# Ten landing slots, later accumulating transfers and a re-ordered DMA queue in the output product of a feed-forward block

## What is computed

```python
def conv_ffn(x, g_norm, w_in, conv_w, conv_b, w_out):
    h = rms_norm(x, g_norm)
    hu = causal_depthwise_conv(h @ w_in, conv_w, conv_b)
    gate, up = jnp.split(hu, 2, axis=-1)
    return (jax.nn.silu(gate) * up) @ w_out
...
        x = x + conv_ffn(x, f_norm[layer], f_w_in[layer], f_conv_w[layer], f_conv_b[layer],
                         f_w_out[layer])
```

## Time and profile before

| what | value |
|---|---|
| median of 3 runs | 2029.73 us (2027.12 to 2032.08) |
| the profiled execution, its own time | 2034.66 us |
| its span | 2032.9 us |
| mean granted TensorE clock | 0.98 |
| TensorE matmuls, share of the span | 96% |
| VectorE / ScalarE / GpSimd | 74% / 46% / 22% |
| output product of layer 0 (first to last matmul start) | 752.74 to 978.61 us |
| output product of layer 1 | 1804.32 to 2029.35 us |

### The profile page before, as it was taken

The page is one execution under the profiler, slowest core; times in us unless marked ns, Lnnn a source line. Parts: engine busy times, 40 slices in busy tenths (PEclk is TensorE's granted clock), DMA queues, the critical chain, the costliest instruction groups (busy, mean ns, idle before and its releaser), DMA issues.

```text
span 2032.9 us, 27966 instructions
## 1 busy us (share of the span) xinstructions
PE 1947.5 (96%) x9704; PEld 1649.4 (81%) x9704; DVE 1503.0 (74%) x2202; ACT 933.9 (46%) x1620; POOL 445.5 (22%) x321
## 2 busy tenths in 40 slices
PE   7999899999999998999999799989999999989999
PEld 7988778788888886888999688867788888867887
DVE  5356658888888875786844688889887887866875
ACT  5233434544444443444412788756444444433443
POOL 0000001333333220020110445532333333310100
PEclk9999999999999998999999799999999999999999
DMA  4111142122222259680112000011222222289761
GB/s 170 43 42 42 52 155 104 62 83 83 83 82 83 83 174 311 192 207 1 42 42 69 15 11 12 22 78 68 84 83 83 83 83 83 83 240 339 142 143 63
DMA packets 62820, 198.99 MB, mean 98 GB/s; under 512 B 5008, under 2 KB 5136, under 8 KB 55568
## 3 DMA queue, kind: packets, MB, share of 16 engines
q1 hardware_dynamic: 48080, 163.29, 22.6%
q0 software_dynamic: 14656, 34.61, 7.9%
HBM read 162.22 MB, written 35.65 MB: 97 GB/s over the span
## 4 chain that ended last, share of the span: by engine, by line
PE 80%; DVE 10%; DMA 4%; ACT 3%; issue 1%; SPq 0%; POOL 0%; DVEq 0%; ACTq 0%
PE banks L2082 26%; PE banks L2084 26%; PE banks L2083 26%; DMA raw<-in_w_f_out 1%; DMA b<-c_scratch 1%; DVE t_lo L1600 1%; DMA c_scratch<-xT 1%; ACT lg L1302 1%; PE banks L2418 1%; DVE t_sum L1840 1%; DVE t_sum L1590 1%; DVE lg L1982 1%; DVE small L1989 1%; DVE fw_lo L1756 1%; DVE xT L1682 1%
## 5 line engine op out<-in xcount | busy, mean ns | idle before, releaser
L2082 PE MATMUL banks<-t_hi,fw_hi 128*128 128x512 f32 x1248 | 488.8, 392 | 11.0 <-issue 11.0
L2084 PE MATMUL banks<-t_hi,fw_lo 128*128 128x512 f32 x1248 | 486.9, 390 | 0.0
L2083 PE MATMUL banks<-t_lo,fw_hi 128*128 128x512 f32 x1216 | 474.6, 390 | 0.0
L2082 PEld LDWEIGHTS banks<-t_hi,fw_hi 128*128 128x128 f32 x1248 | 235.5, 189 | 61.3 <-issue 12.6
L2084 PEld LDWEIGHTS banks<-t_hi,fw_lo 128*128 128x128 f32 x1248 | 235.2, 188 | 49.3
L2083 PEld LDWEIGHTS banks<-t_lo,fw_hi 128*128 128x128 f32 x1216 | 229.4, 189 | 48.1 <-issue 0.5
L2082 PE MATMUL banks<-fw_hi,fw_hi 128*128 128x512 f32 x544 | 215.6, 396 | 22.4 <-DVE fw_lo L1756 22.4
L667 POOL TENSOR_TENSOR nrm<-raw 128x512 f32<-128x512 f32 x40 | 53.6, 1339 | 753.7 <-DVE fw_lo L1643 439.7
L2083 PE MATMUL banks<-fw_lo,fw_hi 128*128 128x512 f32 x544 | 214.4, 394 | 0.0
L2084 PE MATMUL banks<-fw_hi,fw_lo 128*128 128x512 f32 x544 | 214.4, 394 | 0.0
L1133 ACT ACTIVATE fw_hi<-b 128x512 fp32r<-128x512 f32 x154 | 96.9, 630 | 220.8 <-PE banks L2084 209.4
(11 more groups left out here) (196 smaller groups left out, 4208.5 us busy)
## 6 DMA issues: line engine op xcount, KB each, us to landing
raw<-in_w_f_in SPq DMA_DIRECT2D x44, 1024.0 KB, 4.9
c_scratch<-xT SPq DMA_DIRECT2D x44, 512.0 KB, 2.6
raw<-in_w_f_out SPq DMA_DIRECT2D x66, 256.0 KB, 6.6
b<-c_scratch SPq DMA_DIRECT2D x16, 1024.0 KB, 9.0
a_sum<-in_w_f_out POOLq DMA_DIRECT2D x16, 1024.0 KB, 10.4
w_raw<-in_w_ao SPq DMA_DIRECT2D x16, 512.0 KB, 3.5
x_scratch<-xT SPq DMA_DIRECT2D x4, 2048.0 KB, 7.2
xT<-x_scratch SPq DMA_DIRECT2D x8, 1024.0 KB, 9.4
```

The costliest lines, as they stand in the source:

```text
L2082: nc.tensor.matmul(out, w_h, m_h, start=start, stop=False, **kw)
L2083: nc.tensor.matmul(out, w_h, m_l, start=False, stop=False, **kw)
L2084: return nc.tensor.matmul(out, w_l, m_h, start=False, stop=stop, **kw)
```

## The change

`DIRECT = 10`: the direct weight tiles get ten slots in place of four. Slots 0 to 3 are `raw_1` as before, 4 and 5 are the two halves of row 2 of `nrm`, 6 to 9 are `raw_0`. Tile m waits for the split of tile m - 10. Six tiles are requested where four were; tiles 6 to 9 wait for the last weight split of the block's first product (`fw_ready` at `w2`). SyncE's whole order is written anew. The three DMAs that add A22 wait for the splits of step 11, 14 and 17. `token_sum` is called with m - 4 in place of m + 2. The first product's `out_add` comes five steps later. The load of `w_kv` waits for the split of step 51.

```diff
+DIRECT = 10
 ...
+        def direct_slot(m):
+
+            r = m % DIRECT
+            if r < 4:
+                return raw_1[:, r, :]
+            return nrm[:, 2, (r - 4) * SUB:(r - 3) * SUB] if r < 6 else raw_0[:, r - 6, :]
 ...
-                    if m >= 4:
-                        prior = m - 4
+                    if m >= DIRECT:
+                        prior = m - DIRECT
                         sp.wait_ge(fw_ready, w2 + (0, 1, 4)[prior // PAIRS] * PAIRS + prior % PAIRS + 1)
-                    sp.dma_start(raw_1[:, m % 4, :], w_f_out[layer * PAIRS + m % PAIRS][:, block * SUB:(block + 1) * SUB]
-                                 ).then_inc(d_landed[m % 4], 16)
+                    sp.dma_start(direct_slot(m), w_f_out[layer * PAIRS + m % PAIRS][:, block * SUB:(block + 1) * SUB]
+                                 ).then_inc(d_landed[m % DIRECT], 16)
 ...
-                for m in range(4):
+                for m in range(6):
                     direct(m)
                 store(i - 1, 1)
                 store(i - 1, 0)
 ...
                 tokens("b21", 1)
-                for m in (4, 5, 6):
+                sp.wait_ge(fw_ready, w2)
+                for m in range(6, DIRECT):
                     direct(m)
                 sp.wait_ge(prod_full, p2)
                 tokens("b11", 0)
-                direct(7)
-                direct(8)
+                direct(10)
                 store(i, 1)
-                direct(9)
-                direct(10)
+                direct(11)
                 store(i, 0)
-                direct(11)
+                direct(12)
+                direct(13)
                 for r in range(2):
                     sp.wait_ge(c_stored[r], 16 * PAIRS * (layer + 1))
                 tokens("b21", 2)
-                direct(12)
                 tokens("b11", 1)
-                direct(13)
+                direct(14)
                 tokens("b11", 2)
-                direct(14)
+                direct(15)
+                direct(16)
                 back(0, 0)
-                direct(15)
+                direct(17)
                 tokens("b12", 0)
-                direct(16)
-                tokens("b12", 1)
-                direct(17)
-                tokens("b12", 2)
                 direct(18)
                 direct(19)
-                tokens("b22", 0)
+                tokens("b12", 1)
                 direct(20)
                 direct(21)
+                tokens("b12", 2)
+                tokens("b22", 0)
+                direct(22)
                 tokens("b22", 1)
-                direct(22)
+                direct(23)
+                tokens("b22", 2)
                 back(1, 0)
-                direct(23)
                 back(1, 1)
-                direct(24)
-                tokens("b22", 2)
-                direct(25)
+                for m in range(24, 32):
+                    direct(m)
                 back(0, 1)
+                if layer:
+                    for dt in range(4):
+                        result(0, dt)
+                direct(32)
                 if layer == 0:
+                    sp.wait_ge(fw_ready, w2 + 4 * PAIRS + 8)
                     for n in range(2):
                         load(n, w_kv[n])
-                else:
-                    for dt in range(4):
-                        result(0, dt)
-                for m in range(26, 3 * PAIRS):
-                    direct(m)
 ...
                 for g in range(3):
+                    pool.wait_ge(fw_ready, w2 + 12 + 3 * g)
                     pool.wait_ge(a_summed[g], sums + 16)
                     nc.gpsimd.dma_start(tiles(a_sum, g), block(g, A22), accum_op=ALU.add).then_inc(a_summed[g], 16)
 ...
                             gated_lower(m + 2)
-                            token_sum(m + 2)
-                        if m >= PAIRS and 1 <= m % PAIRS <= 4:
-                            out_add(m // PAIRS - 1, m % PAIRS - 1)
+                        if m >= 4:
+                            token_sum(m - 4)
+                        late = 5 if m < 2 * PAIRS else 0
+                        if m >= PAIRS and 1 <= m % PAIRS - late <= 4:
+                            out_add(m // PAIRS - 1, m % PAIRS - late - 1)
```

More of the change, by code:

```diff
@@ L124, in ring_uses @@
 def ring_uses(r, m):
-    return len([i for i in range(m) if i % 4 == r])
+    return len([i for i in range(m) if i % DIRECT == r])
 def split_at(m):
@@ L321, in out_weight @@
             if s in OUT_DIRECT:
-                return raw_1[:, (OUT_DIRECT[s][0] + k) % 4, :]
+                return direct_slot(OUT_DIRECT[s][0] + k)
             return b21[:, k, :] if s == 5 else a_sum[:, k, :]
@@ L424, in build @@
         c_stored = [sem(f"c_stored{r}") for r in range(2)]
-        d_landed = [sem(f"d_landed{s}") for s in range(4)]
+        d_landed = [sem(f"d_landed{s}") for s in range(DIRECT)]
         b_landed = {b: [sem(f"{b}_landed{g}") for g in range(3)] for b in ("b11", "b12", "b21", "b22")}
@@ L521, in direct @@
                     first, block = OUT_DIRECT[(0, 1, 4)[m // PAIRS]]
-                    n = (0, 1, 4)[m // PAIRS] * PAIRS + m % PAIRS
-                    if m >= 4:
-                        prior = m - 4
+                    if m >= DIRECT:
+                        prior = m - DIRECT
                         sp.wait_ge(fw_ready, w2 + (0, 1, 4)[prior // PAIRS] * PAIRS + prior % PAIRS + 1)
-                    sp.dma_start(raw_1[:, m % 4, :], w_f_out[layer * PAIRS + m % PAIRS][:, block * SUB:(block + 1) * SUB]
-                                 ).then_inc(d_landed[m % 4], 16)
+                    sp.dma_start(direct_slot(m), w_f_out[layer * PAIRS + m % PAIRS][:, block * SUB:(block + 1) * SUB]
+                                 ).then_inc(d_landed[m % DIRECT], 16)
                 def tokens(name, g):
@@ L1113, in out_upper @@
                         m = OUT_DIRECT[s][0] + k
-                        act.wait_ge(d_landed[m % 4], 16 * (ring_uses(m % 4, 3 * PAIRS) * layer + m // 4 + 1))
+                        r = m % DIRECT
+                        act.wait_ge(d_landed[r], 16 * (ring_uses(r, 3 * PAIRS) * layer + m // DIRECT + 1))
                     elif s == 5:
```

## The result

The changed kernel takes 2015.59 us (median of 4 runs, 2012.44 to 2017.59), the kernel before in the same comparison 2028.85 us (4 runs). The ratio is 0.9925 (95% interval 0.9912 to 0.9939): faster, by 13.3 us between the medians and 15.2 us by the ratio. In a later comparison with more runs of each it gave 0.9899 (0.9881 to 0.9916), 20.5 us; the two intervals just overlap. The profiled execution has a span of 2013.1 us, 19.8 us less than before.

The account below looks back on a forecast made before the run. Taken to bound: late landings where SyncE's loads share the DMA engines with A22's accumulates, 32.5 us lost in both output products. Gains of 11.0 and 10.8 us, in all 21.8, off 2029.7 give 2007.9 us; range 1998.5 to 2018.

Parts of the forecast that it names:

- rival 2: Output products: congestion only moved, shared rate 120 GB/s, 12 us lost per layer, gain 8 us, 2021 us; chance 0.16.
- What binds: Both output products: TensorE waits on late landings while queues share the DMA engines; 32.5 us lost in all.
- The early part: Output products, steps 0 to 9: stalls removed, step 8 just met; 0 us of stall left (0 to 1.5).
- The new stall: Step 17, behind tile 18: 3.3 us stall plus 1.7 us low clock, 5.0 us per layer (1.3 to 7.3).
- the place "1850": Layer 1's output product: sign that one stall, behind tile 18's landing, would stand near 1850, as near 799 in layer 0.
- The walk: SyncE's queue from 770.6, summed in MB at full, then shared rate: tile 18 lands at 802.4 without gaps, 800.2 taken.
- The later sums and adds: Output products: token sums six steps later and first product's adds at iterations 17 to 20 cost 0 us.
- The gain on GpSimd: Layer 0 near 907: VectorE held 5 us in one instruction by GpSimd's sums, costing about 0.7 us (0 to 1.5).
- The sum: Whole kernel: layer 0 gains 11.0 us, layer 1 10.8 us, in all 21.8 us off a median of 2029.7.
- Rival 1: Output products: nearly all won, tile 18 lands before 797; gain 29 to 32 us, 1999 us; chance 0.20.
- Rivals 3 and 4: Slower through late s = 5 weights (0.05 with other slower ways); SyncE's queue takes no twenty transfers, 2019 us (0.05).
- Rival 3: out_upper(63): s = 5 weights late, over 16 us per layer to be slower, 2032 to 2038 us; 0.05 with other slower ways.

Follow-up runs that it names:

- The run with all edits: Changed kernel with tiles 20 and 21 ahead of b12 group 1, A22 waits later, b21 group 2 ahead of tiles 12 and 13: 2000.87 us, 0.9843.
- with the adds early: Changed kernel with the first product's additions into xT back in iterations 12 to 15: 2012.46 us, 0.9905.
- the gates set later: Changed kernel with the three A22 DMAs waiting for the splits of step 13, 17 and 21 in place of 11, 14 and 17: 2003.26 us, 0.9857.
- the gate alone: Kernel before plus only the A22 DMAs' wait for the splits of step 11, 14 and 17: 2029.87 us, 0.9989.
- without the gate: Changed kernel minus the wait that begins the A22 accumulates later; slots, order and later sums stay: 2030.21 us, 0.9995.

## Why the prediction was right, and where it was off

The forecast was 2007.9 us, the measured median 2015.6, inside the range (1998.5 to 2018); the ratio that belongs to the forecast, 2007.9 / 2029.7 = 0.9893, lies outside the first interval and inside that of the repetition. 2015.6 us is also outside the stretch of 2003 to 2013 that had the highest chance, and by its size alone it could have been rival 2 or 4 in part; the traces decide that it was not. What was right is the mechanism, more than the size.

- *What binds.* Right. All but 0.3 us of the difference of the two profiled spans lies in the two output products, and taking either the gate or the rest away takes the whole gain away.
- *The early part.* Right in kind: the store left at 764.35 (764.9 said), landed in 2.9 us, and steps 3, 5, 6 are in time. Off in size: b21 group 2 was put at 772 to 773 and landed at 774.0, 6.7 us after its issue, because tiles 12 and 13 stood ahead of it. The term was 0 (0 to 1.5); it measured 1.5 us. The run with all edits took the tiles away, and the term with them. It also scatters: with the adds early and the same order up to there, the load took 7.4 us in layer 0 and 5.5 in layer 1, and steps 8 to 10 lost 3.8 and 0.2 us. What moves it was not followed.
- *The new stall.* Right in mechanism and nearly in size: 3.25 us and 1.7 us of low clock, where 3.3 and 1.7 stood. Wrong in place: step 19 behind tile 20, not step 17 behind tile 18. Two errors cancelled. The walk let the accumulates take their share 2 us after their issue, at 778; they took it at 782 (below), so tiles 15 and 16 and most of back(0,0) passed at the full rate and tile 18 landed at 796.8. But the walk stopped at tile 18. Next in the queue stand tile 19 (799.0) and b12 group 1 (806.0, 7 us at what is nearly all shared rate), and only then tile 20: 806.7, and 806.7 + 2.1 = 808.8 is the restart (808.89). The agreement of 3.3 with 3.25 us is luck. So is that of the place "1850": it was said in the frame of before (1804.32 + 17 x 2.72), and the product now begins 10.4 us sooner and stalls two steps later.
- *The later sums and adds.* Right: no wait of ScalarE for a_sum or the s = 5 weights, and the adds cost nothing (6.3 and 6.0 us with them early). The A22 groups landed about 3 to 4 us later than the 788, 796 and 803 said, as their accumulates began later; with 10 us and more to spare it cost nothing. What the prediction did not price is what the later sums bring, since it priced the change as a whole: 5 us per layer.
- *The gain on GpSimd.* The 5 us instruction came at 907.27 (907 said); it met a token sum with slack, so 0.7 us became 0. It returned as 0.3 to 0.8 us at step 56 in four of the variants: it depends on which instruction of VectorE it meets (a lower part in that with the adds early, at 901.45), and what sets that was not followed.
- *The sum.* 21.8 us said; 19.6 us in the two traces, the remaining 2.2 being about step 8's 2 x 1.5 us less the gain's 0.7. On the medians the first comparison shows 13 to 15 us and the second 20 to 23. The step that failed there is the base: "the median to expect is 2029.7 - 21.8" takes it that three or four runs fix a median. Runs of before lie between 2026.0 and 2035.5 us (25 of them on one chip); in the pair of traces above, the difference is mostly the clock in a stage outside the change. The unbroken walk comes to 802.2 by its own terms, not 802.4, which changes nothing.
- *The rivals.* Rival 1's end is what a better order reaches (2000.9 us), not this change. Rival 2 did not occur: SyncE's queue had 128 GB/s beside the accumulates (2.56 MB in 20 us), not 120, and the gates set later leave no new stall. A part of its picture is true, since what is left of the congestion moved to step 19. Rivals 3 and 4 have nothing for them: the s = 5 weights landed at 914.2 and were never waited for, and SyncE ran ahead without trouble: at 777.41 ten of its transfers were on their way, at 815.22 thirteen. It was never more in this trace, so whether the queue takes twenty is not shown. Rival 3's price does not fit the forecast either: against a gain of 21.8 us, 11 us per layer and not 16 would have made the kernel slower.

## What to carry to other kernels

When accumulating DMAs share the engines with a queue of loads, look for what must land last and price everything that stands ahead of it at the shared rate: here 1 MB at 130 GB/s is 8 us, and swapping three lines removed a loss of 5 us per layer. Starting the accumulates later and making their victims less urgent only worked together: the gate alone moved the stall to step 12, the rest alone gathered it at step 8, and neither gained anything. Walk the queue past the first late item to the last due one in the stretch.

## What the runs showed of the hardware that was not expected

An accumulating DMA that is issued while many of SyncE's transfers are under way takes its share late. The first was issued at 777.56; in the DMA window 778:782 only SyncE's queue (and one packet of instructions) appears, at its full rate:
```profile
DMA packets 455, 1.59 MB, mean 397 GB/s; under 512 B 46, under 2 KB 46, under 8 KB 333
...
q1 hardware_dynamic: 454, 1.58, 100.5%
q14 instruction: 1, 0.01, 0.5%
```
With the gates later the same is seen: issued at 778.64, 38 packets of GpSimd's queue by 784. The delay is less than half when SyncE's queue is empty. In the kernel before, the accumulate of A11's second group is issued with none of SyncE's transfers under way, and its first packet comes 2.0 us later, at 842.20:
```profile
840.22 1.27 POOL L707 DMA_DIRECT2D a_sum<-in_w_f_out  x1 [10.18 <-DVE fw_lo L1751]
```
In the changed kernel the accumulate of A11's first group is issued at 819.85 with eleven of them under way, and its first packet comes 4.7 us later. Over the traces, GpSimd's first packets of a burst come 1.5 to 2.7 us after the issue with at most one SyncE transfer under way, and 3.2 to 5.0 us with six or more. Why was not tried.

What the low clock costs does not follow the length of the wait ahead of it. Idle times of 12.4 us (without the gate, step 8), 3.1 us (changed, step 19) and 1.9 us (gate alone, step 19) were followed by 2.4, 1.7 and 1.5 us of lateness in the next step, one of 1.3 us (changed, step 8) by 0.1 us. Behind nearly the same 3.0 us the changed kernel's second trace lost 2.9 us over two steps. The prediction's 1.7 us was the right size, and its low end (0 us behind a stall of 1.3) is what the wait at step 8 shows.
